# A gated DeltaNet layer on one core: its input units in the order k, q, v, z, and K K^T between v's two units

## The reference

```python
proj = h @ w_in                        # 1024 -> q, k, v (3 x 1024), z (1024), b, a (8 + 8)
q, k, v = silu(causal_conv4(qkv))      # a short convolution over time, per channel
q = l2_normalize(q) * 128 ** -0.5;  k = l2_normalize(k)
beta = sigmoid(b);  g = -exp(A_log) * softplus(a + dt_bias)
decay = cumsum(g);  L = exp(decay_i - decay_j) on and below the diagonal
A = strictly_lower(beta_i * (k_i . k_j) * L);  solve (I + A) [U, W] = [beta v, beta k exp(decay)]
Aqk = lower(q_i . k_j * L)
v_new = U - W state;  o = (q exp(decay)) state + Aqk v_new;  the state decays and takes k^T v_new
o = rms_norm(o) * norm_w * silu(z);  out = o @ w_out
```

## Time and profile before

| | |
|---|---|
| median of the runs | 1043.1 us |
| the profiled execution | 1043.19 us |
| its span, from the first to the last instruction | 1041.5 us |
| TensorE busy | 1028.7 us, 99% of the span |
| VectorE, ScalarE, GpSimd busy | 600.5, 526.7, 58.2 us |
| mean granted TensorE clock | 0.998 |

### The profile page before, as it was taken

The page is one execution under the profiler, slowest core; times in us unless marked ns, Lnnn a source line. Parts: engine busy times, 40 slices in busy tenths (PEclk is TensorE's granted clock), DMA queues, the critical chain, the costliest instruction groups (busy, mean ns, idle before and its releaser), DMA issues.

```text
span 1041.5 us, 14317 instructions
## 1 busy us (share of the span) xinstructions
PE 1028.7 (99%) x5290; PEld 869.1 (83%) x5290; DVE 600.5 (58%) x842; ACT 526.7 (51%) x777; POOL 58.2 (6%) x120
## 2 busy tenths in 40 slices
PE   9999999999999999999999999999999999999997
PEld 7888888887888888888888888998997878888886
DVE  5645555467565545546555454686697665554543
ACT  7445343558464345436354353587567555533532
POOL 0000000100000000000000000404204100000000
PEclk9999999999999999999999999999999999999999
DMA  9765565444345564653755565441251257555521
GB/s 329 238 200 164 186 219 201 138 155 122 115 137 193 183 217 164 218 189 119 229 174 176 210 218 177 152 144 42 81 191 73 82 182 240 163 186 211 206 83 41
DMA packets 124302, 175.73 MB, mean 169 GB/s; under 512 B 7360, under 2 KB 97760, under 8 KB 124256
## 3 DMA queue, kind: packets, MB, share of 16 engines
q1 hardware_dynamic: 121552, 172.77, 49.4%
q10 hardware_dynamic: 2704, 2.33, 0.7%
HBM read 174.02 MB, written 1.06 MB: 168 GB/s over the span
## 4 chain that ended last, share of the span: by engine, by line
PE 94%; DVE 4%; ACT 2%; issue 0%; POOL 0%; ACTq 0%; POOLq 0%; DVEq 0%
PE bank L1611 28%; PE bank L1613 27%; PE bank L1612 27%; PE bank L1959 2%; PE bank L1675 2%; PE bank L1953 2%; PE bank L1632 1%; DVE w_lo L1104 1%; PE bank L1882 1%; PE bank L1819 1%; PE bank L1850 1%; PE bank L1749 1%; DVE k_T L1412 0%; DVE q_T L1412 0%; PE bank L2056 0%
## 5 line engine op out<-in xcount | busy, mean ns | idle before, releaser
L1104 DVE TENSOR_TENSOR w_lo<-w_raw,w_hi 128x2048 fp32r<-128x2048 f32 x153 | 348.1, 2292 | 143.1 <-ACT w_hi L713 143.0
L713 ACT ACTIVATE w_hi<-w_raw 128x2048 fp32r<-128x2048 f32 x155 | 293.7, 1918 | 111.8 <-PE bank L1613 111.8
L1611 PE MATMUL bank<-w_hi,xT_hi 128*128 128x512 f32 x784 | 310.5, 396 | 0.8 <-DVE w_lo L1274 0.5
L1613 PE MATMUL bank<-w_hi,xT_lo 128*128 128x512 f32 x784 | 305.7, 390 | 0.0
L1612 PE MATMUL bank<-w_lo,xT_hi 128*128 128x512 f32 x784 | 305.2, 389 | 0.0
L1611 PEld LDWEIGHTS bank<-w_hi,xT_hi 128*128 128x128 f32 x784 | 147.2, 188 | 32.5 <-issue 2.4
L1613 PEld LDWEIGHTS bank<-w_hi,xT_lo 128*128 128x128 f32 x784 | 147.1, 188 | 31.1
L1612 PEld LDWEIGHTS bank<-w_lo,xT_hi 128*128 128x128 f32 x784 | 147.3, 188 | 29.9 <-issue 0.5
L766 ACT ACTIVATE silu_g<-bank,rstd 128x256 f32<-128x256 f32 x88 | 36.9, 471 | 247.0 <-PE bank L1613 247.0
L1611 PE MATMUL bank<-w_hi,hT_hi 128*128 128x512 f32 x352 | 138.3, 393 | 0.0
L1613 PE MATMUL bank<-w_hi,hT_lo 128*128 128x512 f32 x352 | 137.1, 390 | 0.0
(11 more groups left out here) (292 smaller groups left out, 972.3 us busy)
## 6 DMA issues: line engine op xcount, KB each, us to landing
w_raw<-in_ffn_w_gate_up SPq DMA_DIRECT2D x170, 512.0 KB, 4.7
w_raw<-in_ffn_w_down SPq DMA_DIRECT2D x88, 512.0 KB, 4.0
w_raw<-in_gdn_w_in SPq DMA_DIRECT2D x32, 512.0 KB, 4.3
w_raw<-in_attn_w_in SPq DMA_DIRECT2D x12, 512.0 KB, 4.3
w_raw<-in_attn_w_out SPq DMA_DIRECT2D x8, 512.0 KB, 3.7
w_raw<-in_gdn_w_out SPq DMA_DIRECT2D x8, 512.0 KB, 4.2
w_raw<-in_ffn_w_gate_up SPq DMA_DIRECT2D x12, 256.0 KB, 5.2
x_sb<-in_x SPq DMA_DIRECT2D x4, 256.0 KB, 4.4
```

Source lines behind the costliest of these rows:

```text
L713: act.activation(w_hi[u0 % RING][:], w_raw[u0 % RING][:], ACT.Copy).then_inc(hi_ready, 1)
L1104: dve.tensor_tensor(w_lo[u0 % RING][:], w_raw[u0 % RING][:], w_hi[u0 % RING][:].bitcast(F32), ALU.subtract).then_inc(split_ready, 1)
L1611: pe.matmul(out_ap, a[0], b[0], start=start, stop=False, **kw)
L1613: return pe.matmul(out_ap, a[1], b[0], start=False, stop=stop, **kw)
```

## The change

The columns of w_in are streamed in the order k, q, v, z. `part` now counts the order of the stream, and `GDN_PARTS` gives the channel set of a part. The convolutions keep their banks by position, so that k now has q's old banks and the reverse. `FILL_K` comes ahead of `FILL_Q`.

TensorE: k's transposes stand ahead of v's first unit, K K^T stands between v's units, q's transposes stand behind v's second unit and wait until `k_dec` and `k_w` have been taken from banks 4 and 5. In the second group K K^T goes to banks 0 and 1, and TensorE waits for the whole of A ahead of z's first unit, which writes these banks.

VectorE: the diagonal of K K^T follows the second convolution, then k's inverse norm and its scales, then A. The first group's decay differences follow k's scales; the second group's stand ahead of the scaling of q's banks. The splits of units 6 and 7 of a group come later (in the first group unit 6's behind k's scales and unit 7's behind A; in the second both behind A), then v's scaling and convolution, then q's inverse norm.

ScalarE: the root is taken of k's inverse alone, `k_dec` and `k_w` follow it at once. The decays' exps come behind them in the first group, and ahead of the square root in the second. Then come q's squares (which now write into `AT`, not `Y`), v's products, and the copies of A. q's root is taken late in the group, where the square root's table is loaded anyway.

The diff without the declarations of the semaphores (`kq_inv`, `kq_root` and `kq_ssq` become `k_inv`, `q_inv`, `k_root`, `q_root` and `k_ssq`):

```diff
-GDN_COLS = [part * D + g * HG * DK for g in range(NG) for part in range(4)]
+GDN_PARTS = [1, 0, 2, 3]
+GDN_COLS = [part * D + g * HG * DK for g in range(NG) for part in GDN_PARTS]
 ATT_COLS = [D, 0, BANK]
...
 CONV_BANKS = [[(2, 3), (0, 1), (6, 7)], [(0, 1), (2, 3), (6, 7)]]
-KK_BANK, QK_BANK = [2, 3], [2, 3]
+KK_BANK, QK_BANK = [[2, 3], [0, 1]], [2, 3]
 Y_BANK, Z_BANK, XT_BANK = [2, 3], [2, 3], [6, 7]
...
 R_BEFORE = [10, 15]
-FILL_Q, FILL_K, FILL_A, FILL_XO, FILL_AQK, FILL_V, FILL_X, FILL_O, FILLS_G = range(0, 18, 2)
+FILL_K, FILL_Q, FILL_A, FILL_XO, FILL_AQK, FILL_V, FILL_X, FILL_O, FILLS_G = range(0, 18, 2)
 EVACS_G = 12
...
                     for h in (2 * b, 2 * b + 1):
-                        col = (CONV - 1) * 24 + part * 8 + HG * g + h
-                        z = act.activation(cT[part][:, h, :], bank[CONV_BANKS[g][part][b]][:, (h % 2) * SEQ:(h % 2 + 1) * SEQ],
+                        col = (CONV - 1) * 24 + GDN_PARTS[part] * 8 + HG * g + h
+                        z = act.activation(cT[GDN_PARTS[part]][:, h, :], bank[CONV_BANKS[g][part][b]][:, (h % 2) * SEQ:(h % 2 + 1) * SEQ],
                                            ACT.Copy, scale=conv_cols[:, col:col + 1])
...
                 act.wait_ge(conv_sum, HG * (3 * g + part + 1))
-                act.activation(cT[part][:], cT[part][:], ACT.Silu).then_inc(conv_ready, 1)
+                channels = cT[GDN_PARTS[part]]
+                act.activation(channels[:], channels[:], ACT.Silu).then_inc(conv_ready, 1)
...
                 for h in range(HG):
-                    z = act.activation(Y[t][:, h, :], bank[4 + f % 2][:, h * DK:(h + 1) * DK], ACT.Square,
+                    z = act.activation(AT[t][:, h, :], bank[4 + f % 2][:, h * DK:(h + 1) * DK], ACT.Square,
                                        accum_out=sc[:, row, t, h:h + 1])
...
                     z.then_inc(g_evac_k, 1)
-                    for t in range(TT):
-                        g_copy(g, FILL_A + t, AT[t])
...
                 conv_silu(g, 1)
-                for t in range(TT):
-                    squares(g, t, 0, g_evac_act)
+                def decays():
+                    for t in range(TT):
+                        act.wait_ge(decay_diff, TT * g + t + 1)
+                        act.activation(Lm[t][:], Lm[t][:], ACT.Exp, scale=-1.0).then_inc(decay_exp, 1)
+
                 if g == 0:
...
                     act.activation(gates[:, 4], gates[:, 5], ACT.Exp).then_inc(gate_act, 1)
-                for t in range(TT):
-                    act.wait_ge(decay_diff, TT * g + t + 1)
-                    act.activation(Lm[t][:], Lm[t][:], ACT.Exp, scale=-1.0).then_inc(decay_exp, 1)
+                else:
+                    decays()
                 act.activation(spare[:], norm_cols[:, 0:1], ACT.Sqrt)
-                act.wait_ge(kq_inv, g + 1)
-                act.activation(sc[:, RHO:RK + 1], sc[:, 2:4], ACT.Sqrt).then_inc(kq_root, 1)
+                act.wait_ge(k_inv, g + 1)
+                act.activation(sc[:, RK], sc[:, 3], ACT.Sqrt).then_inc(k_root, 1)
+                k_scaled()
+                if g == 0:
+                    decays()
+                for t in range(TT):
+                    squares(g, FILL_Q + t, 0, g_evac_act)
                 conv_products(g, 2)
-                k_scaled()
+                for t in range(TT):
+                    g_copy(g, FILL_A + t, AT[t])
                 for n in range(8, 10):
...
                 act.activation(spare[:], norm_cols[:, 0:1], ACT.Sqrt)
+                act.wait_ge(q_inv, g + 1)
+                act.activation(sc[:, RHO], sc[:, 2], ACT.Sqrt).then_inc(q_root, 1)
                 copy(U_psum, TT * g + 2, Y[1][:], U_BANK[1], U_ready)
...
                 n = 4 * g + part
+                channels = cT[GDN_PARTS[part]]
                 for shift in range(1, CONV):
...
                             dve.wait_ge(conv_first, 2 * (3 * g + part) + h // 2 + 1)
-                        col = (CONV - 1 - shift) * 24 + part * 8 + HG * g + h
+                        col = (CONV - 1 - shift) * 24 + GDN_PARTS[part] * 8 + HG * g + h
                         src = bank[CONV_BANKS[g][part][h // 2]]
                         z = dve.scalar_tensor_tensor(
-                            cT[part][:, h, shift:SEQ], src[:, (h % 2) * SEQ:(h % 2 + 1) * SEQ - shift],
-                            conv_cols[:, col:col + 1], cT[part][:, h, shift:SEQ], ALU.mult, ALU.add)
+                            channels[:, h, shift:SEQ], src[:, (h % 2) * SEQ:(h % 2 + 1) * SEQ - shift],
+                            conv_cols[:, col:col + 1], channels[:, h, shift:SEQ], ALU.mult, ALU.add)
                         if shift == CONV - 1:
...
                 conv(g, 0, not g)
+                def decay_differences():
+                    for t in range(TT):
+                        dve.wait_ge(R_loaded[t], 16 * (g + 1))
+                        for h in range(HG):
+
+                            z = dve.tensor_scalar(Lm[t][:, h, :], Lm[t][:, h, :],
+                                                  gates[:, 2, t, HG * g + h:HG * g + h + 1], 0.0,
+                                                  ALU.subtract, ALU.max)
+                        z.then_inc(decay_diff, 1)
+
                 if g:
...
                     split_lo(U_GDN + 8 * g + 5)
+                    decay_differences()
                 if g == 0:
...
                 conv(g, 1, False)
-                split_lo(U_GDN + 8 * g + 6)
-                for t in range(TT):
-                    dve.wait_ge(R_loaded[t], 16 * (g + 1))
-                    for h in range(HG):
-
-                        z = dve.tensor_scalar(Lm[t][:, h, :], Lm[t][:, h, :],
-                                              gates[:, 2, t, HG * g + h:HG * g + h + 1], 0.0,
-                                              ALU.subtract, ALU.max)
-                    z.then_inc(decay_diff, 1)
-                split_lo(U_GDN + 8 * g + 7)
-                conv_scale(g, 2)
                 for t in range(TT):
...
                     for h in range(HG):
-                        z = dve.scalar_tensor_tensor(v_beta[:, t, h, :], bank[KK_BANK[t]][:, h * P:(h + 1) * P], 1.0,
+                        z = dve.scalar_tensor_tensor(v_beta[:, t, h, :], bank[KK_BANK[g][t]][:, h * P:(h + 1) * P], 1.0,
                                                      ident[:], ALU.mult, ALU.mult, accum_out=sc[:, 1, t, h:h + 1])
-                    z.then_inc(kq_ssq, 1)
-                dve.wait_ge(g_evac_act, EVACS_G * g + 2)
-                dve.wait_ge(kq_ssq, TT * (g + 1))
-                dve.tensor_scalar(sc[:, 2], sc[:, 0], float(DK), float(DK) * EPS, ALU.mult, ALU.add)
+                    z.then_inc(k_ssq, 1)
+                dve.wait_ge(k_ssq, TT * (g + 1))
                 after(dve.tensor_scalar(sc[:, 3], sc[:, 1], EPS, None, ALU.add))
-                dve.reciprocal(sc[:, 2:4], sc[:, 2:4]).then_inc(kq_inv, 1)
-                dve.wait_ge(kq_root, g + 1)
+                dve.reciprocal(sc[:, 3], sc[:, 3]).then_inc(k_inv, 1)
+                dve.wait_ge(k_root, g + 1)
                 dve.wait_ge(gate_act, 6)
...
                                          ALU.mult, ALU.mult).then_inc(k_scales, 1)
+                if g == 0:
+                    split_lo(U_GDN + 8 * g + 6)
+                    decay_differences()
                 for t in range(TT):
...
                     for h in range(HG):
-                        z = dve.scalar_tensor_tensor(Y[t][:, h, :], bank[KK_BANK[t]][:, h * P:(h + 1) * P],
+                        z = dve.scalar_tensor_tensor(Y[t][:, h, :], bank[KK_BANK[g][t]][:, h * P:(h + 1) * P],
                                                      sc[:, 5, t, h:h + 1], Lm[t][:, h, :], ALU.mult, ALU.mult)
                     z.then_inc(A_ready, 1)
+                if g:
+                    split_lo(U_GDN + 8 * g + 6)
+                split_lo(U_GDN + 8 * g + 7)
+                conv_scale(g, 2)
                 conv(g, 2)
+                dve.wait_ge(g_evac_act, EVACS_G * g + 2)
+                after(dve.tensor_scalar(sc[:, 2], sc[:, 0], float(DK), float(DK) * EPS, ALU.mult, ALU.add))
+                dve.reciprocal(sc[:, 2], sc[:, 2]).then_inc(q_inv, 1)
                 for t in range(TT):
...
                                   ALU.add).then_inc(O_ready, 1)
+                dve.wait_ge(q_root, g + 1)
                 after(dve.tensor_tensor(sc[:, 9], sc[:, RHO], sc[:, RHO], ALU.mult))
...
                 t = f % 2
-                if f < 2:
+                if f < FILL_Q:
                     if g:
...
                 elif f < FILL_A:
+                    pe.wait_ge(g_evac_k, TT * g + t + 1)
+                elif f < FILL_XO:
                     pe.wait_ge(g_evac_act, EVACS_G * g + t + 1)
-                elif f < FILL_XO:
-                    pe.wait_ge(g_evac_k, TT * g + t + 1)
                 else:
...
                               start=True, stop=True).then_inc(cum_psum, 1)
+                pe.wait_ge(conv_ready, 3 * g + 1)
```

(47 more changed lines are left out.)

## The result

The changed kernel takes 1050.7 us (median of six runs, 1049.9 to 1051.3) against 1043.1 before (six runs, 1042.9 to 1043.3). The ratio is 1.0071 (95% interval 1.006 to 1.0082): it is slower by 7.6 us. The forecast was 1048.3 with a range to 1050.8. The direction and the waits of the mechanism held, and the median lies in the range, but only by 0.1: two of the six runs are above it. It lies in rival A's stretch (1049.9 to 1051.4): TensorE's clock fell, which the forecast had at nothing.

What follows compares the result with a forecast made beforehand. TensorE, busy 99% of the span, bounds the kernel, so only its waits count. Second group +4.34, first group +0.78, split beside GpSimd +0.1 give +5.2: 1048.3 us against 1043.1, range 1046.0 to 1050.8.

Steps and rivals of the forecast that it cites:

- rival A: TensorE's clock falls in the second group's new stop, adding 1.6 to 3.1 us, for 1049.9 to 1051.4; chance 0.11.
- step 1: Second group: k's transposes, now ahead of v's first unit, wait for ScalarE's first SiLU until 768.31; 1.64 us lost.
- steps 3 to 5: Second group: VectorE has k's inverse at about 780.8; ScalarE's table loads and exps put the root at 783.55, A at 784.29.
- steps 6 and 7: Second group: q's transposes start at 785.70 (3.21 lost, then 0.63); z's first unit waits for its split until 788.79 (1.67 lost).
- The first group: Heads 0 to 3: a third exp table load on ScalarE makes z's SiLU late, +0.78 us, bounds 0 to 1.3.
- The clock: TensorE's granted clock in the second group's new stop: the likeliest case added 0 us for a fall.
- The split beside GpSimd: VectorE's critical splits fall under GpSimd's X products in both groups: +0.1 us taken, range 0 to +0.5.
- The table loads: ScalarE's loads taken at 1.28 us each; at the skill's 2.7 the kernel would be some 4 us slower still.

Runs made afterwards that it cites:

- experiment 2: Changed kernel plus 42 idle filler transposes ahead of q's transposes, and k's transposes back behind v's first unit, both in the second group: 1048.5 us, ratio 1.0054.
- experiment 4: Changed kernel with the decays' exps ahead of q's products on ScalarE in the second group: 1048.0 us, ratio 1.0051 to the kernel before.
- experiment 3: Changed kernel with the split of z's first unit moved from behind A to behind k's inverse on VectorE, second group: 1047.8 us, ratio 1.0043.
- experiment 6: Changed kernel plus filler transposes, with the first group's ScalarE split of unit 9 moved from ahead of z's SiLU into the solver's loop: 1047.9 us, ratio 1.005.
- experiment 1: Changed kernel plus 28 idle filler transposes on TensorE ahead of q's transposes in the second group: 1048.5 us, ratio 1.0049.

## Why the prediction was right, and where it was not

- *Start at k's SiLU (step 1).* 1.64 forecast; TensorE stood still 1.55 there (from 766.67 to 769.36 less 1.14). But experiment 2 shows that this wait cost nothing by itself. As terms of a sum the numbers were right; as prices of single edits, which is how "1.64 lost" reads, they were not: without this wait the next one is longer by as much.
- *ScalarE's chain (steps 3 to 5).* Root 783.55 forecast, 784.70 - 1.14 = 783.56 measured; A at 784.29 against 784.27. Shown as the cause by experiment 4.
- *q's transposes and z's unit (steps 6 and 7).* 785.70 and 788.79 forecast, 785.67 and 788.77 measured. That it is the split and not A which releases z's unit is shown by experiment 3.
- *The first group.* 0.78 forecast, 0.69 measured; shown by experiment 6 to be ScalarE's lateness at z's SiLU.
- *The clock.* This is the term that was wrong. The likeliest case had it at 0, and I gave rival A 0.11. It fell in all six runs, and in experiment 1 its absence is worth 2.3 to 2.5 us (1.6 to 3.1 was A's price). That the median still lies within the range is owed to the range, which was drawn to the middle of A, and to little else. My argument against it, that a unit ran at full pace behind the stop of 1.4 before, compared a stop of 1.4 with 5.5 us of standing still in 6.3: there was no row of before that bore on such a stretch, so this was no evidence. Nor did it take the whole 6.3: the clock was down 2.8 us into the first stop, and in experiment 3, which has no second stop, it fell at 786.6, right behind the first. 1048.3 without the clock's term is what the runs with the clock up took, 1048.2 to 1048.9.
- *The split beside GpSimd.* I took +0.1, in the belief that both engines would be held up. The split was not slowed (4.48 for two, 2.24 each), and GpSimd was: one product took 5.27 instead of 1.0, and ended 0.85 behind the second split. In the first group, under one split (708.87 to 711.15), it took 3.07 and ended 0.86 behind it.

```profile
708.94 3.07 POOL L674 TENSOR_TENSOR X<-X,ident 128x256 f32<-128x256 f32 x1
...
787.55 5.27 POOL L674 TENSOR_TENSOR X<-X,ident 128x256 f32<-128x256 f32 x1
```

The Trainium skill's rule (Trainium Architecture, The Big Picture, section "What this means for kernel authors") that the two exclude each other agrees with these rows. It cost nothing here, since TensorE takes X only at 805.16.

- *The table loads.* Each took 1.28, and the next instruction followed at once (the exps at 782.13 behind the load of 780.83). The Trainium skill (ScalarE: Activation LUTs, "Table sets: the hidden batching unit") has about 2.7 for one; the measurement decides. Its advice to do all exps, then all roots, is about the number of loads; here their number in the second group didn't change, only their place on the chain.

What stays open: on which pattern of stops the clock falls. With experiment 4's kernel it fell in four runs of five. With the filler (experiments 1, 2 and 6) it stayed up in ten runs of fifteen; the other five, by their times and means, lost it and took 1049.2 to 1050.3. The one of them that was profiled doesn't say why.

## What to carry to other kernels

Before a stage is moved forward, lay out the chain that must be ready for it, with each table load and each split in the queues of the other engines, and compare its end with the new need, not with the old. Taking out one wait wins nothing while a later one is released by another chain (experiment 2): price an edit by the last releaser. And where a change makes TensorE stand still for longer than any row of before shows, the clock needs a term of its own in the sum. The small steps of the change (k's scaling ahead of v's products, v's scaling behind A) were worth 1.8 to 2.0 us without the reordering, and every operation that is put off must be followed to the next thing queued behind it.

## What the runs showed of the hardware

A stop of 3.2 us brought the granted clock from 2.4 to 1.2 GHz in every run of the changed kernel (six runs, means 0.995 and 0.996) and of experiment 3 (five runs, 0.997); in the two profiles it fell 2.8 and 3.5 us after the stop began. It stayed at 1.2 GHz for 6.8 us in the one and for 3.4 us in the other, where the stop of 1.1 us behind it was gone and z's unit began 1.4 us sooner. There the unit took 6.46 us instead of 7.11. Filler of 28 transposes, about 3 us, in the long stop was worth 2.3 to 2.5 us. GpSimd's products that began beside VectorE's splits ended 0.85 us behind the last of them (5.27 and 3.07 us instead of 1.0), and the splits weren't slowed (2.24 each).
